# The first two chunks of the mixers' input projection as one pair of 178 + 178 columns, and the start reordered

## The reference

```python
for l in range(DEPTH):                                   # DEPTH = 2
    h = rms_norm(x, mix_norm_g[l])                       # x: [1, 256, 1024]
    proj = jnp.einsum("bsd,dc->bsc", h, w_in[l])         # w_in[l]: [1024, 2660]
    moba_p, mla_p, sb_p, ssm_p = _split(proj, (MOBA_COLS, MLA_COLS, SB_COLS, SSM_COLS))
    ...
```

## Time and profile before

| what | value |
|---|---|
| median of 3 runs | 2599.91 us (2598.31 to 2601.88) |
| the profiled execution: its time | 2599.22 us |
| its span in the trace | 2597.3 us |
| PE busy | 2562.4 us (99%), 18462 matmuls |
| DVE busy, ACT busy | 1688.5 us (65%), 1322.2 us (51%) |
| DMA | 460.26 MB, mean 177 GB/s |
| ACT split of a 2048-column chunk | about 1.91 us |
| DVE split of a 2048-column chunk | 2.29 us |

### The profile page before, as it was taken

How to read it: one execution, slowest core, us unless ns; L and a number is a source line. 1 busy time by engine, 2 the same in 40 slices (tenths; PEclk the granted TensorE clock), 3 DMA queues, 4 the chain that set the end, 5 groups by cost and what they waited for, 6 DMA issues and landing times.

```text
span 2597.3 us, 43244 instructions
## 1 busy us (share of the span) xinstructions
PE 2562.4 (99%) x18462; PEld 2378.8 (92%) x18462; DVE 1688.5 (65%) x2364; ACT 1322.2 (51%) x1938; POOL 156.9 (6%) x228
## 2 busy tenths in 40 slices
PE   8999999999999999999999999999999999999998
PEld 7999899998998989989988998998899899897997
DVE  6878567785665766656656665666766566566663
ACT  6756466654544554444455444444554454355542
POOL 2100011000000000000011000002000000000000
PEclk9999999999999999999999999999999999999999
DMA  7267552665766547567664766665457567563863
GB/s 223 86 175 215 170 160 84 181 193 162 209 189 200 181 134 198 184 182 195 187 218 139 198 192 178 192 190 192 147 152 198 185 179 196 191 207 99 219 186 122
DMA packets 568313, 460.26 MB, mean 177 GB/s; under 512 B 12346, under 2 KB 529290, under 8 KB 568122
## 3 DMA queue, kind: packets, MB, share of 16 engines
q1 hardware_dynamic: 562615, 441.91, 58.0%
q0 software_dynamic: 4656, 15.30, 1.8%
q10 hardware_dynamic: 851, 0.28, 0.0%
HBM read 456.37 MB, written 1.10 MB: 176 GB/s over the span
## 4 chain that ended last, share of the span: by engine, by line
PE 90%; DVE 5%; ACT 3%; DMA 1%; issue 1%; POOL 0%; DVEq 0%; POOLq 0%; SPq 0%; ACTq 0%
PE ps L899 28%; PE ps L764 16%; PE ps L766 16%; PE ps L765 16%; PE ps L718 3%; PE ps L720 3%; PE ps L719 3%; DVE wlo L1882 1%; ACT h_hi L1303 1%; DMA raw<-in_w_in 1%; PE ps L643 1%; DVE h_lo L1943 1%; ACT prob L1303 1%; ACT whi L1303 1%; PE ps L1001 1%
## 5 line engine op out<-in xcount | busy, mean ns | idle before, releaser
L1882 DVE TENSOR_TENSOR wlo<-raw,whi 128x2048 fp32r<-128x2048 f32 (+1 forms) x419 | 956.6, 2285 | 499.9 <-ACT whi L1303 499.2
L1303 ACT ACTIVATE whi<-raw 128x2048 fp32r<-128x2048 f32 (+1 forms) x421 | 802.9, 1910 | 793.2 <-DMA raw<-in_ff_w_in 420.2
L764 PE MATMUL ps<-h_hi,whi 128*128 128x256 f32 x3584 | 1006.9, 281 | 0.0
L765 PE MATMUL ps<-h_lo,whi 128*128 128x256 f32 x3584 | 1003.3, 280 | 0.0
L766 PE MATMUL ps<-h_hi,wlo 128*128 128x256 f32 x3584 | 1003.0, 280 | 0.0
L764 PEld LDWEIGHTS ps<-h_hi,whi 128*128 128x128 f32 x3584 | 673.7, 188 | 5.0 <-issue 5.0
L766 PEld LDWEIGHTS ps<-h_hi,wlo 128*128 128x128 f32 x3584 | 674.9, 188 | 0.0
L765 PEld LDWEIGHTS ps<-h_lo,whi 128*128 128x128 f32 x3584 | 673.4, 188 | 0.0
L899 PE MATMUL ps<-whi,hid_lo 128*128 128x512 f32 x880 | 296.2, 396 | 0.0
L899 PE MATMUL ps<-whi,hid_hi 128*128 128x512 f32 x880 | 295.2, 394 | 0.0
L899 PE MATMUL ps<-wlo,hid_hi 128*128 128x512 f32 x880 | 294.5, 394 | 0.0
(11 more groups left out here) (312 smaller groups left out, 2135.5 us busy)
## 6 DMA issues: line engine op xcount, KB each, us to landing
raw<-in_ff_w_in SPq DMA_DIRECT2D x176, 1024.0 KB, 6.1
raw<-in_ff_w_out SPq DMA_DIRECT2D x88, 1024.0 KB, 5.0
raw<-in_ffn_w_in SPq DMA_DIRECT2D x44, 1024.0 KB, 6.0
raw<-in_a_w_qkv SPq DMA_DIRECT2D x24, 1024.0 KB, 5.2
raw<-in_ffn_w_out SPq DMA_DIRECT2D x22, 1024.0 KB, 4.9
raw<-in_w_in SPq DMA_DIRECT2D x19, 1024.0 KB, 5.3
raw<-in_c_w_qkv SPq DMA_DIRECT2D x12, 1024.0 KB, 5.1
raw<-in_w_out SPq DMA_DIRECT2D x8, 1024.0 KB, 4.9
```

What stands on the lines that cost most here:

```text
L764: e.matmul(out, hi, m.h_hi[:, k, :], start=(k == 0), stop=False)
L765: e.matmul(out, hi, m.h_lo[:, k, :], start=False, stop=False)
L1303: return self.nc.scalar.activation(*a, **k)
L1882: self.e.tensor_tensor(chunk_view(m.wlo[:, slot, :], c), chunk_view(m.raw[:, slot, :], c), chunk_view(m.whi[:, slot, :], c).bitcast(F32), ...
```

## The change

- `IN_PIECES`: the first two chunks have 178 columns each (174 + 4 dt in the second).
- `Tensor.pair` makes both together: one matmul has 2 x 178 = 356 moving columns, read from two slots; token tile t goes to bank 2 + t, so chunks 2 and 3 (banks 0 and 1) wait for no eviction (`paired`). `chunk_done` rises by 2 at the end of the pair, and `pair_half` tells ACT that tile 0 is done.
- In `head` the turning of x tile 1 comes behind the sixth feature block of the pair's tile 0. In layer 0 the parameter rows are turned between the two tiles, in banks 0 and 1.
- ACT evicts a token tile of 356 columns with one instruction, and takes the squares before it splits chunk 5. In layer 0 it splits chunk 3 behind the first eviction.
- Start: SP loads x and the halves of both chunks; the dt columns are loaded from ACT's queue as its third DMA, and the first split waits for them. The 512 KB table comes behind chunk 3. POOL makes `rstd` first, then issues its loads, the later of them behind chunk 3's landing.

```diff
+PAIR = (QR + KVR + ROPE + 4) // 2
+IN_PIECES = ((C_CQ, [(C_CQ, PAIR)]), (C_CQ + PAIR, [(C_CQ + PAIR, PAIR - 4), (W_DT, 4)]),
...
     def start(self):                                      # Sync
-        for t, signal in ((0, s.first_landed), (1, s.landed[0])):
+        for t in range(TT):
             e.dma_start(m.x[:, t, :], d.x[0, t * P:(t + 1) * P, :]).then_inc(s.x_in[t], 16)
-            e.dma_start(raw[:, 4 * t:4 * t + 4, 0:n], w[:, 4 * t:4 * t + 4, col:col + n]).then_inc(signal, 16)
+            for b in range(2):
+                col, n = IN_PIECES[b][1][0]
+                e.dma_start(raw[:, b, 4 * t:4 * t + 4, 0:n],
+                            w[:, 4 * t:4 * t + 4, col:col + n]).then_inc(s.first_landed if t == 0 else s.landed[b], 16)
         self.load_rows(1)
...
-        for b in range(1 if l == 0 else 0, IN_CHUNKS):    # Sync.mix
+        for b in range(2 if l == 0 else 0, IN_CHUNKS):
             self.chunk(b, 0, pick)
-            if l == 0 and b == 1:
+            if l == 0 and b == 3:
                 e.dma_start(m.consts[:, CONST["upto"][0]:], ...).then_inc(s.tables_in, 16)
...
+    def pair(self, turn=None):                            # Tensor
+        e, m, s = self.e, self.m, self.s
+        c = self.c0
+        whi, wlo = (a[:, c % SLOTS:c % SLOTS + 2, :].rearrange("p s (k c) -> p k s c", k=KT) for a in (m.whi, m.wlo))
+        self.at(s.bank_free, self.b0)
+        if c == 0:
+            e.wait_ge(s.first_lo, 1)
+        else:
+            e.wait_ge(s.split_lo, c + 2)
+        for t in range(TT):
+            out = view(m.ps[:, 2 + t, 0:2 * PAIR], a=2)
+            for k in range(KT):
+                if k % 4 == 0:
+                    self.wait_features(2 * t + k // 4 + 1)
+                if (c, t, k) == (0, 0, 4):
+                    e.wait_ge(s.split_lo, 2)
+                if turn is not None and (t, k) == (0, 6):
+                    turn()
+                hi, lo = m.h_hi[:, k, t * P:(t + 1) * P], m.h_lo[:, k, t * P:(t + 1) * P]
+                w_hi, w_lo = whi[:, k, :, 0:PAIR], wlo[:, k, :, 0:PAIR]
+                e.matmul(out, hi, w_hi, start=(k == 0), stop=False)
+                e.matmul(out, hi, w_lo, start=False, stop=False)
+                ins = e.matmul(out, lo, w_hi, start=False, stop=(k == KT - 1))
+            if t == 0:
+                ins.then_inc(s.pair_half, 1)
+                if turn is None:
+                    self.turn_rows()
+        ins.then_inc(s.chunk_done, 2)
...
+        self.paired = True                                # Tensor.mix
         if r == 1:
             self.begin_product()
-            chunk(0)
-            self.turn_rows()
-            chunk(1)
+            self.pair()
+            e.wait_ge(s.rows_kept, 1)
         chunk(2)
...
+        e.dma_start(dt, ...[:, :, W_DT:W_DT + 4]).then_inc(s.first_landed, 16)   # Scalar.start
         self.load_rows(0)
...
+        if half == 0:                                     # Scalar.split_first
+            self.e.wait_ge(s.first_landed, 48)
+        else:
+            self.e.wait_ge(s.landed[0], 16)
+            self.e.wait_ge(s.landed[1], 16)
+        for b in range(2):
+            ins = self.act(first_half(m.whi, b, half), first_half(m.raw, b, half), ACT.Copy)
+        ins.then_inc((s.first_hi, s.split_hi)[half], 1 + half)
...
-        self.split(0, 0)                                  # Scalar.mix
+        if l > 0:
+            self.split(0, 0)
         e.wait_ge(s.rstd, TT * self.rounds["norm"])
-        keep(0)
+        keep_tile(0)
+        if l == 0:
+            self.split(0, 0)
         self.split(1, 0)
-        keep(1)
-        self.split(2, 0)
+        keep_tile(1)
         e.wait_ge(s.bank_free, self.b0 + 2)
         self.act(m.c_squares, proj[:, :, C_CQ:C_KR], ACT.Square).then_inc(s.c_sq, 1)
+        self.split(2, 0)
...
     def first_norm(self, gain):                           # Pool
         for t in range(TT):
             self.rstd_x(t)
+        e.wait_ge(s.landed[1], 16 * landings(1))
+        e.dma_start(m.ext[:, 0:2 * REL + 1], d.a_rel_bias.rearrange("l h c -> (l h) c")).then_inc(s.ext_in, 16)
+        self.layer_rows(0)
```

More of the change, by code:

```diff
@@ L148, in __init__ @@
         self.first_landed = new("first_landed")
+        self.pair_half = new("pair_half")
         self.first_hi = new("first_hi")
@@ L393 @@
     gates_ring = False
+    paired = False
     a0 = 0
@@ L669, in turn_rows @@
         for r in range(ROW_TILES):
-            ins = e.transpose(m.ps[:, 2 + r // 4, (r % 4) * P:(r % 4 + 1) * P], m.rows[:, r, :], m.ident)
+            ins = e.transpose(m.ps[:, r // 4, (r % 4) * P:(r % 4 + 1) * P], m.rows[:, r, :], m.ident)
         ins.then_inc(s.rows_turned, 1)
@@ L696, in chunk_start @@
         else:
-            self.at(self.s.bank_free, self.b0 + max(b + 1 - self.ring, 0))
+            self.at(self.s.bank_free, self.b0 + (0 if self.paired and b < 4 else max(b + 1 - self.ring, 0)))
     def tokens_tile(self, b, t, w=256, features=False, between=None, gates=False):
@@ L729, in tokens_chunk @@
         self.last.then_inc(self.s.chunk_done, 1)
+    def pair(self, turn=None):
[26 more added lines that the diff above has]
+        ins.then_inc(s.chunk_done, 2)
     def head(self, turn, kind):
         gates = kind in ("swiglu", "ffn1")
-        widths = IN_WIDTH[0:HEAD] if kind == "mix1" else [256] * HEAD
         self.begin_product()
+        if kind == "mix1":
+            self.pair(turn)
+            return
         for t in range(TT):
@@ L739, in head @@
                     self.chunk_start(b, 0)
-                self.tokens_tile(b, t, widths[b], features=(b == 0), between=turn if (t, b) == (0, HEAD - 1) else None, gates=gates)
+                self.tokens_tile(b, t, features=(b == 0), between=turn if (t, b) == (0, HEAD - 1) else None, gates=gates)
                 if t == TT - 1:
@@ L1208, in mix @@
         self.ring = RING
+        self.paired = False
         self.advance(IN_CHUNKS)
@@ L1385, in first_norm @@
                      accum_out=self.m.ss[:, t:t + 1]).then_inc(self.s.squares, 1)
-        self.split(1 - AHEAD, 0)
+        self.split(2 - AHEAD, 0)
         self.keep_rows()
-        self.split(2 - AHEAD, 0)
     def keep_rows(self):
@@ L1955, in first_norm @@
         self.turn_lo(1, gain)
-        for b in range(1 - AHEAD, 0):
-            self.split(b, 0)
+        self.split(2 - AHEAD, 0)
         self.e.wait_ge(self.s.rows_kept, 1)
@@ L1963, in split_first @@
         self.e.wait_ge((s.first_hi, s.split_hi)[half], 1)
-        part = slice(1024 * half, 1024 * half + 1024)
-        self.e.tensor_tensor(m.wlo[:, 0, part], m.raw[:, 0, part], m.whi[:, 0, part].bitcast(F32),
-                             ALU.subtract).then_inc((s.first_lo, s.split_lo)[half], 1)
+        for b in range(2):
+            ins = self.e.tensor_tensor(first_half(m.wlo, b, half), first_half(m.raw, b, half), first_half(m.whi, b, half).bitcast(F32),
+                                       ALU.subtract)
+        ins.then_inc((s.first_lo, s.split_lo)[half], 1 + half)
     def weigh_sum(self, t, half, weight):
@@ L2690, in row @@
         return self.e.dma_start(dst, src.unsqueeze(0).to_broadcast([P] + list(src.shape)))
-    def start(self):
-        e, m, s, d = self.e, self.m, self.s, self.d
-        e.wait_ge(s.landed[1], 16 * landings(1))
-        e.dma_start(m.ext[:, 0:2 * REL + 1], d.a_rel_bias.rearrange("l h c -> (l h) c")).then_inc(s.ext_in, 16)
-        self.layer_rows(0)
     def layer_rows(self, l):
@@ L2707, in layer_rows @@
                 self.e.dma_start(m.w_ukv[:, :], d.mla_w_ukv[l]).then_inc(s.w_in_small, 16)
+                if l == 0:
+                    self.e.wait_ge(s.landed[3], 16 * landings(3))
             self.row(m.wide_(name), src[name]).then_inc(s.wide_in if n < N_FIRST else s.wide_late, 16)
@@ L2913, in landings, with first_half @@
 def landings(c):
-    return sum(2 if k in NARROW else 1 for k in range(c % SLOTS, c + 1, SLOTS))
+    return sum(2 if k > 1 and k in NARROW and k - 1 in NARROW else 1 for k in range(c % SLOTS, c + 1, SLOTS))
+def first_half(a, b, half):
+    return a[:, b, :].rearrange("p (k c) -> p k c", k=KT)[:, 4 * half:4 * half + 4, 0:PAIR]
 def chunk_view(ap, c):
```

27 lines of the change are left out of this document (13 added, 14 removed).

## The result

The changed kernel takes **2607.47 us** (median of 8 runs, 2606.02 to 2610.89) where the kernel before takes 2599.86 in the same series (8 runs, 2598.31 to 2601.88): **1.0029 times as long, 95% interval 1.0020 to 1.0038, 7.6 us slower**. The forecast was 2597.2 with a range to 2600.5: wrong, and on the wrong side. The profiled execution has a span of 2605.3 (before 2597.3) and a time of 2607.14.

The account below looks back on a forecast made before the run. The prediction took PE's matmul work as the bound, with chunk 5's load chain deciding what arrives. Gains of 0.8 us (second mixer) and 1.9 (first) summed to 2.7: 2597.2 against 2599.91, range 2593.3 to 2600.5.

Parts of the forecast that it names:

- (a): First mixer's start: first halves landed at 7.9 instead of 6.61, with the dt load on ACT's queue costing about 1 us.
- (e): First mixer: chunk 5, issued at 22.3 instead of 17.64, lands at 29.2, the middle between 27.5 and 30.6.
- (d): First mixer, behind the pair: no wait for ACT's eviction, POOL's rstd done about 19.8, chunks 2 and 3 from 22.3 to 33.65.
- The second mixer: PE pauses 1.2 us before tile 1, then waits 1.6 for chunk 5's chain; gain 0.8 us of 3.2.
- rival 4: First mixer's start: the dt load starves, landing about 19.5; (b) to (f) come 11.6 later, time 2606.8; chance 0.07.
- (b): First mixer's start: splits of 1424 columns instead of 1024, so PE starts at 12.3, 2.1 later than before.
- (c): First mixer's pair: lower clock for 3.3 us after PE's start, 12 matmuls to 15.85; pair done at 22.2.
- (f): First mixer: 7.8 us after chunk 5's landing PE goes on, at 37.1 instead of 41.01, 3.9 us gained.
- (g): First mixer: PE pauses from 33.65 to 37.1 and the low clock behind it loses 2.0 us, leaving a gain of 1.9.
- rival 2: First mixer: chunk 5 lands undisturbed at 27.5, pause of 1.7 without loss; 6.4 us gained in all, 2593.5; chance 0.15.
- rival 1: First mixer: the clock stays up through PE's pause, 2.0 us more gained, time 2595.2; chance 0.27.
- rival 3: First mixer: the DMA engines are the bound, chunk 5 lands at 31 or later whatever the order; 2600 to 2601; chance 0.08.

Follow-up runs that it names:

- e1: The changed kernel with layer 0's dt columns zeroed by POOL instead of loaded: 2604.86 us, +6.4 against the kernel before.
- e2: The changed kernel with POOL's 13 loads issued ahead of its rstd, as in the kernel before: 2602.80 us, +4.3 against the kernel before.
- e9: e7 with ScalarE's evictions and squares and VectorE's sums and products ahead of the splits of chunks 4 and 5: 2594.27 us, -5.1 against the kernel before.
- e11: The changed kernel with 132 already satisfied waits at the head of PE's queue: 2607.18 us, +7.8 against the kernel before.
- e8_before_sums: The kernel before, without the pair, with ScalarE's squares and VectorE's sums and products ahead of chunk 5's splits: 2598.13 us, -0.5 against the kernel before.
- e5: The changed kernel with the dt load issued by SP, behind x tile 0 and ahead of the first halves: 2605.09 us, +6.4 against the kernel before.
- e6: The changed kernel with VectorE's sums, means and products cn ahead of chunk 5's split: 2600.89 us, +2.2 against the kernel before.
- e7: The changed kernel with the edits of e2, e5 and e6 together: 2596.76 us, -1.9 against the kernel before.

## Why the prediction was wrong, point by point

The steps that failed are (a), the dt load, priced at 1 us of waiting where it cost 3.4, and (e), chunk 5's time under way, taken as 6.9 us where it was 10.5; a loss of 3.5 us in the gMLP stage had no term at all.

**The matmul of 356 columns** was right: 0.165 us a step for 0.163, 0.297 at the lower clock for 0.296. **No bank wait** (d) was right too: POOL's rstd was done at 20.8 for 19.8, and chunk 2 started at once.

**The second mixer** was right in its mechanism and near in size. PE starts tile 1 after a pause of 0.97 (1.2 predicted), chunk 5 decides, the cn transposes wait 1.65 (1.6). Gain 0.74 at 397.10 (5.09 to 4.35), 0.8 predicted.

**(a) failed, by size.** Forecast: first halves split from 7.9. The part without dt was right, 7.42 by e1. The dt load was priced at 1 us from a stretch in which such pieces ran in a row on SP's own queue; it cost 3.4. This was rival 4, whose mechanism came at a quarter of its size (10.81 is 2.9 behind the forecast, the rival had 11.6). No row of before shows what it does beside a full queue. The trace of after does; the stretches 6 to 8 and 8 to 10:

```profile
q1 hardware_dynamic: 345, 0.64, 98.9%
q10 hardware_dynamic: 349, 0.01, 12.7%
```

```profile
q1 hardware_dynamic: 661, 0.47, 85.7%
q10 hardware_dynamic: 666, 0.08, 30.3%
```

From 6 to 11 the two queues advance one packet for one packet (284 to 284 from 10 to 11), whatever their sizes. A piece of 16 bytes waits for one of SP's each time, and from 6 to 8 there are 121 over 2 KB, rows of x tile 1, among those: 0.64 MB in 345. While that holds, 1024 pieces take as long as 1024 of SP's packets, bytes and all. It does not hold from 4 to 6, where SP's queue has 872 and ACT's 255; why was not tried. The Trainium skill's "DMA: Bandwidth & Descriptors", section "Queues, rings and completion order", has this rule, turns between queues by the packet; from 6 on the trace agrees, 345 to 349 and 661 to 666. The prediction quoted it and drew the wrong end from it ("in with the first halves"): it counted no packets. Counted, x tile 0 and the first halves are 128 + 1024 packets, and the dt pieces stand behind the constants in their own queue: at one for one they end only when x tile 1 has begun.

**(b) and (c)** were right as differences: from first split to PE start 4.5 us (4.4 predicted). The low clock lasted 5.2 us from PE's start (15.30 to about 20.5), not 3.3, 18 matmuls instead of 12, which is 0.8 more. So the pair was done at 26.2 for 22.2: 2.9 of (a), 0.8 of the clock.

**(e) failed, by size, and is the larger error.** Chunk 5 took 10.5 us from its issue (26.2 to 36.7) where 6.9 had been taken and 8.3 was the upper end. The bound was built on the share of POOL's queue over 8 us in which both queues had work and SP's had been first. Here POOL's loads were issued from 20.8 on and had the engines when chunk 5 came; e2 shows it: with these loads moved away PE goes on 4.7 us earlier. That an issue of 13 loads was moved was priced; that it was moved onto the one transfer on which PE's chain hung was named in the text and then averaged away ("taken 29.2, the middle").

**(f)** was right: 7.8 us from landing to PE (36.73 to 44.51). **(g)** was right: pause, then low clock; it cost 1.6 (3.50 to 5.09) for 2.0 predicted. The page quoted there (the Trainium skill's "TensorE: Matmul & The Clock Gate") agrees with it here: a pause of 6.82, then 27 matmuls at 0.63.

Chunk 5 issued 3.9 late (a to c) and 3.6 longer under way (e) is 7.5 behind the forecast's 37.1, 44.6; measured 44.51. By the point of decision in rival 4 (11.8) a landing at 10.8 should still have been a gain; with (e) as it was, it wasn't. That the result is within 1 us of that rival's 2606.8 is chance: its own term came at a quarter of its size, and (e) and 3.5 us from a place that no part of the prediction had made up for the rest. Two figures don't add up as they stand: rival 2 with a third of rival 1 is 0.24, not 0.23, and the range's lower end is 2593.3 where rival 2 has 2593.5; neither matters.

**Not foreseen: the gMLP stage**, +2.0 us of wait and +1.5 of low clock behind it (1388.14 to 1393.10 at 0.66), over 1000 us behind the last edited instruction, in the second mixer. The sentence "what is gained shifts the rest as a whole" failed here. The change takes 96 matmuls and as many weight loads out of PE's program (18462 to 18366 of each by the pages), so all later instruction loads fall elsewhere.

**What the rivals of the experiments say.** The DMA engines' bytes (rival 3) do not bound this stage: e9 passes at 34.89. What bound it was order, in three queues: POOL's loads ahead of chunk 5, VectorE's and ScalarE's waits for chunk 5 ahead of work that was ready. The 3.3 us of PE time per mixer were real in both; the pair brought them to 37.7, and the queues behind it took them back.

## What to carry to other kernels

Before pricing shorter work on the bounding engine, list for each in-order queue behind it what stands ahead of the next thing that engine needs; a split that waited for a DMA ahead of a reduction that was ready held PE here for 6.8 us. Many small pieces on a second queue can cost as many packets of the busy queue, not their bytes: here 3.4 us, and 1.1 on the same queue, in a row. When one part of a change moves a set of loads, price it against the one transfer that the chain hangs on, at its worst position, not with a mean share.

## What the hardware showed unexpectedly

- An instruction load of 16 KB held one of the 16 DMA engines for 1.0 to 2.3 us; inside a transfer that something waits for, it made that wait 0.9 to 2.0 us longer (seven kernels with, seven without). So a kernel's time can depend on the number of instructions ahead: with 132 waits that do nothing e9's 2594.27 became 2590.66 (1.0 us of it at this wait), and in e11 they only moved the loss. Such waits count half: 60, 132 and 196 of them added 30, 66 and 98 instructions to the pages' counts.
- The same pauses can be followed by either clock. Behind the attention near 1880, with waits of 0.38 to 0.63 us in both, the windows of the kernel before and of e8_before_sums (stretch, length, busy, granted clock, DMA share, GB/s) are:

```profile
1882.70:1887.70 5.00, 4.96 (x24) 1.00 0.01 3
```

```profile
1879.40:1884.40 5.00, 4.96 (x15) 0.50 0.02 3
```

  e8 was 3.4 us ahead of the kernel before in front of this place and only 0.9 us ahead after it. The wait for b_uv does the same: in the 5 us behind it the granted clock was 0.66 to 0.71 after waits of 3.35, 2.61, 2.25 and 2.40 us (the changed kernel, e1, e2, e5) and 1.00 after 2.91, 2.18 and 2.35 (e6, e7, e9), so a longer wait was not always the one that cost the clock. What decides was not tried. A difference of 2.5 us between single profiles can come from this alone.
- What stays open: why a POOL packet held an engine so much longer than one of SP's (79 of them took 39.3% of 4 us, 459 of SP's 36.9%) was not tried.
